# Leaving out three of five groups of filler matmuls in the scans of a hybrid RWKV-7 / Gated DeltaNet step

## The reference

```python
def step(S, inp):                      # Gated DeltaNet, one chunk, per head
    q_n, k_n, u_n, w_n, qk_n, gl_n = inp
    v_new = u_n - jnp.einsum('bhck,bhkv->bhcv', w_n, S)
    o = jnp.einsum('bhck,bhkv->bhcv', q_n, S) + jnp.einsum('bhij,bhjv->bhiv', qk_n, v_new)
    S = S * gl_n[..., None, None] + jnp.einsum('bhck,bhcv->bhkv', k_n, v_new)
    return S, o
...
def step(S, inp):                      # RWKV-7, one token, per head
    r_t, w_t, k_t, v_t, a_t, b_t = inp
    sa = jnp.einsum('bhvk,bhk->bhv', S, a_t)
    S = S * w_t[:, :, None, :] + sa[..., None] * b_t[:, :, None, :] + v_t[..., None] * k_t[:, :, None, :]
    return S, jnp.einsum('bhvk,bhk->bhv', S, r_t)
```

## Time and profile before

| | us |
|---|---|
| median of 3 runs | 2735.81 |
| lowest and highest | 2732.69, 2738.3 |
| span of the profiled execution, first to last instruction | 2729.5 |
| PE busy in it | 2186.6 (80%) |
| DVE, ACT, POOL busy | 995.2, 533.5, 260.1 |
| mean granted clock of TensorE | 0.871 of full speed |

### The profile page before, as it was taken

The page is one execution under the profiler, slowest core; times in us unless marked ns, Lnnn a source line. Parts: engine busy times, 40 slices in busy tenths (PEclk is TensorE's granted clock), DMA queues, the critical chain, the costliest instruction groups (busy, mean ns, idle before and its releaser), DMA issues.

```text
span 2729.5 us, 39969 instructions
## 1 busy us (share of the span) xinstructions
PE 2186.6 (80%) x13000; PEld 1561.1 (57%) x13000; DVE 995.2 (36%) x2443; ACT 533.5 (20%) x1291; POOL 260.1 (10%) x646
## 2 busy tenths in 40 slices
PE   6989998899996997999999989666457777777760
PEld 1256665788885876777878777433234434444430
DVE  0020312455555564655555565555201111111114
ACT  1110146222333122222222122121000000000001
POOL 0000001111112111111110111000100000000001
PEclk8989989999997898988888889777678889888885
DMA  7611060000000000000000000200299999999982
GB/s 259 219 58 58 21 237 26 16 0 0 0 0 9 0 0 8 0 0 0 0 0 0 0 0 0 85 16 15 44 312 384 383 384 386 381 382 384 384 303 100
DMA packets 167707, 331.21 MB, mean 121 GB/s; under 512 B 24500, under 2 KB 41012, under 8 KB 167540
## 3 DMA queue, kind: packets, MB, share of 16 engines
q1 hardware_dynamic: 153686, 306.08, 31.0%
q0 software_dynamic: 4720, 14.95, 1.8%
q10 hardware_dynamic: 9264, 9.72, 1.1%
HBM read 301.35 MB, written 29.38 MB: 121 GB/s over the span
## 4 chain that ended last, share of the span: by engine, by line
PE 43%; DVE 12%; SPq 12%; DMA 11%; issue 6%; ACT 2%; POOL 1%; DVEq 0%; POOLq 0%; ACTq 0%; PEldq 0%
SPq L459 6%; PE ps L304 6%; PE ps L293 6%; PE ps L300 5%; DMA fm<-in_expert_up 4%; SPq L461 4%; DMA ring<-in_expert_up 3%; PE ps L824 3%; PE ps L275 3%; PE ps L774 3%; PE ps L566 2%; DVE ring L338 2%; DVE ring L1522 1%; SPq L458 1%; PE ps L675 1%
## 5 line engine op out<-in xcount | busy, mean ns | idle before, releaser
L293 PE MATMUL ps<-ring 128*128 128x128 f32 x1440 | 241.0, 297 | 59.2 <-DVE ring L338 47.3
L293 PEld LDWEIGHTS ps<-ring 128*128 128x128 f32 x1440 | 189.4, 194 | 95.9 <-DVE ring L338 74.6
L304 PE MATMUL ps<-ring 128*128 128x128 f32 x1440 | 229.4, 284 | 0.1
L824 PE MATMUL ps<-ring,z_tm 128*64 128x256 f32 x1216 | 165.2, 439 | 51.9 <-DMA ring<-in_expert_up 50.8
L316 ACT COPY ring<-ps 128x256 f32<-128x256 f32 x360 | 134.0, 372 | 363.1 <-PE ps L293 360.1
L824 PE MATMUL ps<-fm,z_tm 128*64 128x256 f32 x1152 | 158.9, 444 | 53.3 <-DMA fm<-in_expert_up 52.1
L335 DVE COPY_PREDICATED ring<-tab,ps 128x256 f32<-128x256 int32 x300 | 131.9, 440 | 184.7 <-PE ps L300 183.4
L304 PEld LDWEIGHTS ps<-ring 128*128 128x128 f32 x1440 | 196.0, 198 | 4.7 <-ACT ring L316 2.1
L515 PE MATMUL ps<-hT,ring 128*128 128x320 f32 x704 | 193.3, 437 | 3.6 <-PE ps L515 1.1
L300 PE MATMUL ps<-ring 128*128 128x128 f32 x1200 | 194.4, 287 | 0.5
L338 DVE COPY_PREDICATED ring<-tab,ps 128x256 f32<-128x256 int32 x360 | 159.3, 443 | 55.8 <-PE ps L304 55.3
(11 more groups left out here) (335 smaller groups left out, 2857.4 us busy)
## 6 DMA issues: line engine op xcount, KB each, us to landing
ring<-in_expert_gate SPq DMA_DIRECT2D x19, 2048.0 KB
ring<-in_expert_up SPq DMA_DIRECT2D x19, 2048.0 KB
hT<-in_expert_down SPq DMA_DIRECT2D x19, 2048.0 KB, 21.8
fm<-in_expert_gate SPq DMA_DIRECT2D x18, 2048.0 KB
fm<-in_expert_up SPq DMA_DIRECT2D x18, 2048.0 KB
fm<-in_expert_down SPq DMA_DIRECT2D x18, 2048.0 KB, 21.8
ring<-in_ada_w SPq DMA_DIRECT2D x12, 2048.0 KB, 7.9
ring<-in_w_in SPq DMA_DIRECT2D x7, 2048.0 KB, 7.8
```

What stands on the lines that cost most here:

```text
L293: m = nc.tensor.matmul(ps[d][:, P * hh:P * (hh + 1)], lt(s_), i_x[:, s_, :], start=True, stop=True)
L304: m = nc.tensor.matmul(ps[4 + d][:, P * hh:P * (hh + 1)], i_y[:, s_, :], i_xt[:, s_, :], start=True, stop=True)
L824: m = nc.tensor.matmul(ps[bank][BT * h:BT * (h + 1), 0:256], e_xT[u][:, k, :], w_[:, k, 256 * h:256 * (h + 1)], start=k == 0, stop=k == KD ...
```

## The change

Three of the five calls of `keep_clock` are left out: the four fillers at the end of a Gated DeltaNet iteration, the four between the corrections and the y products of an RWKV iteration, and the eight at its end. The ten after the transposes of a Gated DeltaNet iteration (L602) and the five after those of an RWKV iteration (L683) stay. Nothing else is touched; no result depends on the fillers.

```diff
--- before.py
+++ after.py
@@ -625,7 +625,6 @@
                     nc.tensor.matmul(ps[3][:, P * s_:P * (s_ + 1)], g_qk[:, s_, P:2 * P], g_w[:, s_, P:2 * P], start=True, stop=False)
                     m = nc.tensor.matmul(ps[3][:, P * s_:P * (s_ + 1)], g_t1[:, s_, :], st, start=False, stop=True)
                 m.then_inc(*S.tick("t2"))
-                keep_clock(6, 4)
 
             pe.wait_ge(zeroed, 3)
             with pe.Fori(0, 2) as hp:
@@ -727,7 +725,6 @@
                         nc.tensor.matmul(zo, r_ktm[:, s_, :], v, start=False, stop=False)
                         m = nc.tensor.matmul(zo, r_t1[rows, d, :], r_zin[rows, d, :], start=False, stop=True)
                 m.then_inc(*S.tick("t2"))
-                keep_clock(0, 8)
 
             with pe.Fori(0, FT) as ft:
                 rwkv_pe(ft, ft, (0, 0))
```

## The result

The change made the kernel slower: a median of 2746.88 us (11 runs, 2740.1 to 2752.09) against 2737.03 us for the kernel before (11 runs, 2732.69 to 2744.42), a ratio of 1.0035 with an interval of 1.0023 to 1.0046. The forecast of 2719 us and its range to 2739 us were missed. The profiled execution has a span of 2742.1 us, 12.6 us more than before, and a granted clock of 0.853 instead of 0.871.

The account below looks back on a forecast made before the run. The prediction took a PE-led chain through VectorE and ScalarE, partly at the lower clock in the RWKV scan, as the bound: span 2729.5 - 31.4 direct gain + 15 clock cost = 2713, median 2719 us; 8-in-10 range 2704 to 2739.

Parts of the forecast that it names:

- the DeltaNet fillers at 0: End of a DeltaNet iteration: fillers hidden in PE's wait for the state copy, cost 0, at most 32 us if the clock fell.
- the end part: RWKV iteration from the end of the state products to the next start: from 3.11 to 1.53 us, 28.4 us gained.
- L714 and L591 0.06 and 0.05 us behind their releasers: Sign: first y product (L716 before) starts 0.06 us after VectorE's L1547, DeltaNet's L591 0.05 us after state copy L1440.
- the first part: RWKV iteration from its start (L669) to the first y product: stays between some 33 and 34 us, cost 0.
- The 1 us for fillers that hold up L716: Before the y products of an RWKV iteration: direct gain of 0 to 4.6 us, taken as 1.
- What the clock takes back: RWKV y and state products: clock falls earlier without full-size fillers around them, costing 15 us, between 0 and 71.
- the middle part: RWKV iteration from the first y product to the end of the state products: from a mean 7.15 to 7.90 us.
- the prediction's own bounds of 6.3 and 10.7 us: Four groups each of y and state products, all at the upper clock level (6.3 us) or the lower (10.7 us).
- The second half of the argument there: With the fillers behind the state products gone, nothing lifts the clock until the next iteration's score products; no separate size.
- iteration 6: RWKV iteration with the longest of 18 y-to-state-product stretches, 8.65 us; the forecast 7.90 lies between the mean and it.
- the third rival: Wait before y products drops the clock after their first group: 9.98 us, 2761 us in all, deciding from 8.72; chance 0.13.
- the 6.3 us between span and median: Whole kernel: the median of the runs lies 6.3 us above the profiled span, so 2713 us became 2719.

## Why the prediction was wrong

**Right:** the DeltaNet fillers at 0 (ratio 1.0008 alone); the end part (1.62 us, forecast 1.53), worth 18 x 1.49 = 27 us where 28.4 were taken; L714 and L591 0.06 and 0.05 us behind their releasers; the first part at 33.3 us although the score products start at the lower level in all 18 iterations. The 1 us for fillers that hold up L716 is too small to be seen in any run.

**The step that failed is "What the clock takes back".** Its mechanism was right, the clock falls earlier in the y products; its size was not: the middle part was put at 7.90 us, 20 x 0.75 = 15 us, and it measured 9.25, 20 x 2.10 = 42 us. By the prediction's own bounds of 6.3 and 10.7 us, (7.15 - 6.3) / 4.4 = 19% of these products ran at the lower level before, 36% was forecast, and (9.25 - 6.3) / 4.4 = 67% it became: of 6.3 us of work some 5.1 ran at the upper level before, and 2.1 after. With 42 us in place of 15 the prediction's sum gives 2746 us, and 2746.88 was measured; that it fits within 1 us is luck, since a mean of one execution is good to a few tenths, or some 5 us of time. The second half of the argument there, fillers gone behind the products, had little weight: without the end fillers alone it is 30% (7.60 us), without the four ahead alone 70% (9.37 us).

The size was taken from iteration 6 as the worst of 18. But all 18 had four fillers ahead of their y products, so their spread told how the clock varies with that cover and nothing of what happens without it. What came about is nearest to the third rival: a wait of 1.1 us, then an early fall, in iteration 12 about at the end of the first group, on average after 2.1 us of work, or some two groups. Its break-even of 8.72 us was passed, its 9.98 us was reached in iteration 12 (10.03) but not in the mean, so the time is 2747 and not 2761 us. "8.65 was the worst of 18" was the reason given against it, and was no reason.

A second point is the 6.3 us between span and median. In every execution with both on record the time is 1.8 to 1.9 us above the span. So the profiled execution before took some 2731.4 us, less than any of its 11 runs, and the other 4.4 us say only that it was a quick one. Its 7.15 us are therefore on the low side (7.40 in the kernel without the DeltaNet group, whose RWKV code is the same); with 7.40 the cost would be 20 x 1.85 = 37 us, and 15 too little all the same.

The Trainium skill (TensorE: Matmul & The Clock Gate, "Why this matters for your kernels") names idle gaps of TensorE between bursts of matmuls as what drops the clock, and the gaps that it names are longer than the two waits opened here. The runs show that a shorter one can matter: with 1.1 us idle ahead of the y products the middle part takes 9.25 us, with four fillers there and the end fillers gone 7.60. Opening the wait of 1.6 us at the end of an iteration, on the other hand, made the kernel 0.86% faster.

**The groups do not add up.** Alone they changed the time by +0.47%, -0.86% and +0.08%, which sums to -0.31%; together they gave +0.35%. Part of this is seen: without the four ahead alone, the end fillers gave back 1.26 us of every first part, 33.34 to 32.08; with those gone as well, nothing does, and 20 x 1.26 us is 25 us or 0.9%, enough for the difference.

**What stays open:** why the y products let the clock fall at all while PE is busy throughout (8.65 us of 8.65 at a clock of 0.67), and what it is in a filler that holds it. Half of the rows and half of the columns both lose part of the effect, but the runs don't rank the two. Nor did any run change the length of the loop and leave the fillers alone, so it is not shown how much of a mean comes from the pattern into which the clock settles: with half of the rows, for one, the middle parts take turns at some 8.2 and 7.3 us.

## What to carry to other kernels

Judge each group of fillers by the place it stands in. Fillers inside a wait that is there anyway cost nothing here, and right ahead of small products on the chain they can be worth much (here 20 x 1.6 us between none and four); fillers that outlast the wait delay the chain by their overrun, and have to earn that at the next stage. The price of taking cover away is not to be read from the spread of rows that all have the cover: bound it by the whole of what it covers, and test the groups one by one and together, for one can do another's work.

## What had not been expected of the hardware

- Two fillers of 0.3 us each in a wait of 1.1 us lowered the middle part from 9.25 to 7.88 us, more than twice their own time.
- Four fillers of half the size, in rows or in columns, left the kernel some 0.3% slower than four full ones (0.9947 and 0.9945 against 0.9914), though an instruction takes 272 to 276 ns in all of them.
- The clock can settle into a pattern that repeats with the loop: without the four fillers alone, the middle parts of iterations 4 to 18 are 9.36 to 9.38 us long, at a clock of 0.60, and the first parts of 5 to 18 are 31.82 to 31.84 at 1.00. With the end fillers gone as well the middle parts reach from 7.82 to 10.37 us.
